# Prompt attention: where the value products stand in each quarter of TensorE's program

## The reference, cut to what matters

```python
lg = jnp.einsum('bqghd,bwgd->bghqw', qs, k_win) + tab[t5_bucket(d_win)].transpose(2, 3, 0, 1)
p_win = masked_softmax(lg, m_win)
o_win = jnp.einsum('bghqw,bwgd->bqghd', p_win.astype(v_win.dtype), v_win)
g = jax.nn.sigmoid(gts.astype(jnp.float32)).astype(q.dtype)[..., None]
return g[:, :, 0] * o_cmp + g[:, :, 1] * o_sel + g[:, :, 2] * o_win
```

## Time and profile before

| what | value |
|---|---|
| median of three runs | 1658.26 us (1655.5 to 1662.54) |
| profiled execution, its own time | 1658.38 us |
| its span | 1656.5 us |
| PE busy over the span | 1527.3 us (92%), 10098 matmuls |
| DVE, ACT, POOL busy | 720.8 us, 605.5 us, 201.3 us |
| prompt attention, window 865 to 1346 us | 481 us, PE busy 462.08 |
| granted TensorE clock, mean | 0.969 of full speed |

### The profile page before, as it was taken

One profiled execution on the slowest core, in us unless ns is written; L12 is line 12 of the kernel. 1 busy time (PEld: TensorE's weight loads), 2 busy tenths in 40 slices (PEclk: granted clock), 3 DMA queues, 4 the chain that ended last, 5 costly groups with the idle time before them and its releaser, 6 DMA issues.

```text
span 1656.5 us, 25563 instructions
## 1 busy us (share of the span) xinstructions
PE 1527.3 (92%) x10098; PEld 1321.3 (80%) x10098; DVE 720.8 (44%) x1773; ACT 605.5 (37%) x1231; POOL 201.3 (12%) x380
## 2 busy tenths in 40 slices
PE   5997999999999999959959999999999988799996
PEld 1887999999999999958847777777777766588884
DVE  2540221313123131245557677667676654543221
ACT  2430111110111111124456676666666645521110
POOL 1104000000000000021011122122121131000000
PEclk9999999999999999979979999999999999799998
DMA  9707432332222323187120121111011049662320
GB/s 345 127 27 270 114 103 78 78 90 65 77 78 69 99 53 89 40 267 242 57 85 26 33 75 30 31 44 39 27 47 32 20 152 292 205 193 91 100 67 20
DMA packets 164936, 164.62 MB, mean 99 GB/s; under 512 B 48685, under 2 KB 146029, under 8 KB 159505
## 3 DMA queue, kind: packets, MB, share of 16 engines
q1 hardware_dynamic: 150800, 96.66, 21.9%
q0 software_dynamic: 14016, 66.32, 11.8%
HBM read 131.27 MB, written 35.83 MB: 101 GB/s over the span
## 4 chain that ended last, share of the span: by engine, by line
PE 84%; DVE 6%; DMA 5%; ACT 2%; issue 2%; SPq 1%; POOL 0%; DVEq 0%; ACTq 0%; POOLq 0%
PE PS L975 33%; PE PS L1314 11%; PE PS L1130 8%; PE PS L1098 7%; PE PS L1076 4%; PE PS L1023 4%; PE PS L1077 3%; DMA wr<-in_w_in 2%; PE PS L937 1%; PE PS L938 1%; PE PS L939 1%; PE PS L1170 1%; DMA wor<-in_w_out 1%; DMA adaw<-in_ada_w 1%; PE PS L1015 1%
## 5 line engine op out<-in xcount | busy, mean ns | idle before, releaser
L975 PE MATMUL PS<-hhi,wh 128*128 128x352 f32 x1152 | 251.2, 326 | 9.1 <-issue 8.5
L975 PE MATMUL PS<-hhi,wl 128*128 128x352 f32 x1152 | 248.7, 323 | 0.0
L975 PE MATMUL PS<-hlo,wh 128*128 128x352 f32 x1152 | 248.4, 324 | 0.0
L1479 ACT ACTIVATE pr<-PS,nm 128x640 f32<-128x640 f32 (+7 forms) x256 | 179.8, 704 | 81.9 <-DVE nm L1815 78.1
L975 PEld LDWEIGHTS PS<-hhi,wh 128*128 128x128 f32 x1152 | 196.0, 189 | 13.0 <-issue 11.6
L975 PEld LDWEIGHTS PS<-hhi,wl 128*128 128x128 f32 x1152 | 198.2, 188 | 0.0
L975 PEld LDWEIGHTS PS<-hlo,wh 128*128 128x128 f32 x1152 | 196.0, 188 | 0.0
L1499 ACT ACTIVATE ptt<-PS 128x512 f32<-128x512 f32 x222 | 128.0, 596 | 73.0 <-PE PS L1098 72.8
L1098 PE MATMUL PS<-ident,pr 128*128 128x128 f32 x1056 | 147.3, 274 | 0.0
L1692 DVE TENSOR_TENSOR wl<-wr,wh 128x1024 fp32r<-128x1024 f32 x48 | 58.6, 1220 | 187.5 <-ACT wh L1395 187.0
L1130 PE MATMUL PS<-ptt,kvt 128*64 128x256 f32 x1056 | 136.1, 389 | 1.1 <-DVE ptt L1855 0.7
(11 more groups left out here) (317 smaller groups left out, 2314.2 us busy)
## 6 DMA issues: line engine op xcount, KB each, us to landing
wr<-in_w_in SPq DMA_DIRECT2D x32, 512.0 KB, 7.6
adaw<-in_ada_w SPq DMA_DIRECT2D x8, 1024.0 KB, 9.7
wr<-in_w_in SPq DMA_DIRECT2D x32, 256.0 KB, 3.7
qb<-q_stacked SPq DMA_DIRECT2D x32, 256.0 KB, 3.1
mr<-mixed SPq DMA_DIRECT2D x16, 512.0 KB, 3.9
mixed<-ych POOLq DMA_DIRECT2D x8, 528.0 KB, 3.3
z_attn_silu<-zab POOLq DMA_DIRECT2D x8, 528.0 KB, 2.9
xb<-in_x_prompt POOLq DMA_DIRECT2D x8, 512.0 KB, 7.8
```

Of the source, the lines that this page charges most:

```text
L975: ins = pe.matmul(PS[:, bank + c, 0:CH], a[kind % 2][:, k, :], b[:, k, c * CH:(c + 1) * CH], start=(k == 0 and b is hhi and a is wh), stop ...
L1479: act.activation(pr[r][:, h, 0:k], score_cols(b0, w), ACT.Exp, scale=-1.0, bias=nm[:, r, h:h + 1], accum_out=rsum[:, r, h:h + 1]).then_inc ...
```

## The change

In each quarter `values` moves from behind the turns to a place between the scores and the turns (and ahead of `turn_factors`). In the last two quarters all tiles held are taken, whatever their number; as the quarter's own tiles are not turned yet at that point, these are the tiles of earlier quarters. In the first two quarters it is, as before, the tiles of the window before. The other engines' programs are the same.

```diff
                 for h, part in enumerate(slots(w)):
                     if w + 2 < NI:
                         scores(w + 2, h)
+                    go = sum(x[0] < w for x in held) if h < 2 else len(held)
+                    for x in held[:go]:
+                        values(*x)
+                    held = held[go:]
                     if w % 2 and h == 0:
                         turn_factors(w // 2)
                     for t in part:
                         turn_p(w, t)
                         held.append((w, t))
-                    old = [x for x in held if x[0] < w]
-                    go = len(old) if h < 2 else len(held) - 1 if len(held) >= 5 else 0
-                    for x in held[:go]:
-                        values(*x)
-                    held = held[go:]
             for x in held:
                 values(*x)
```

## The result

The changed kernel takes 1709.21 us (median of four runs, 1702.72 to 1715.84) against 1656.9 us for the kernel before in the same comparison: a ratio of 1.0305 with a 95% interval of 1.0281 to 1.0329. It is 52 us slower. The direction was forecast, the size was not: I had said 1683 us and a range up to 1700.

What follows compares the result with a forecast made beforehand. PE alone was taken to set the pace with large tiles. +10.9 + 11.4 + 2 - 3.0 = +21.3 us there and +4 for small ones made +25 us on 1658.26: 1683 us, range 1660 to 1700.

Steps and rivals of the forecast that it cites:

- The visits: Runs of value products between other PE work: 100 become 168, 0.33 us each before, 0.30 after; +10.9 large, +6.5 small tiles.
- the rival with the full drain: Every entry into value products from scores pays the dearer price, 13.4 us more in all: 1697 us, chance 0.08.
- The 0.17 us from turns to values: Cost of entering value products behind eight transposes: 0.96 us when values follow against 0.79 when scores follow.
- The wait for sel_ev: Odd windows' first product, right behind the third quarter's scores, waits for DVE's selected_o: +11.4 us large tiles, 10.6 small.
- r_ev: Even windows' first product waits for it; the rest of the second quarter and the third's scores hide it: no cost.
- The copies: Values of tiles turned in the same quarter no longer wait for DVE's copy: 3.0 us gone.
- the end of those rows as a sign of being right: In the chain of waits, rows of L1130 (value products) waiting for ptt would be gone.
- Bank waits and small windows: Scores' 16.8 us of bank waits absorb most of 6.5 us visits and 10.6 us sel_ev: +4 us, bounds -17 and +17.
- The 2 us for late exponentials in large windows: ACT's exponentials come later and are wanted sooner: an eighth of a microsecond in 16 even windows, bounds 0 and 5.

Runs made afterwards that it cites:

- the two experiments on them: Changed kernel with values issued behind the turns again: 1679.11 us, ratio 1.0113; kernel before with half the products between a quarter's two turns: 1673.26 us, ratio 1.0097.
- newest held back: Changed kernel, but tiles turned in the quarter just before wait one quarter longer and the first two quarters issue values behind the turns: 1685.57 us, ratio 1.0155.

## Why the prediction was wrong in size

**The visits: right.** The counts are 100 and 168. Both prices show up in the kernel after, here in window 6 (timeline of PE):

```profile
919.58 0.39 PE L1076 MATMUL PS<-ksh,qb 128*128 128x512 f32 x1
919.81 0.40 PE L1077 MATMUL PS<-ksl,qb 128*128 128x512 f32 x1
920.14 0.65 PE L1130 MATMUL PS<-ptt,kvt 128*64 128x256 f32 x4
920.72 1.09 PE L1098 MATMUL PS<-ident,pr 128*128 128x128 f32 x8
921.57 0.42 PE L1076 MATMUL PS<-kwh,qb 128*128 128x384 f32 x1
```

From scores to values it is 0.33 us where scores follow each other by 0.23: 0.10 us to enter, also behind 512 columns, where I had 0.09 from 384. That decides against the rival with the full drain. The Trainium skill (TensorEngine Tiling, Key Properties) says that a change of tiling mode drains the TensorE: the trace agrees that each change costs. The Trainium skill's page TensorE: Matmul & The Clock Gate (Single matmul latency) gives about 175 ns for a drain; the 0.10 us measured here is less. The eight turns behind a visit take 0.85 us against 0.79: 0.06, where I had 0.05. So the visits are +17 us as summed, and the two experiments on them, +19 us for 68 and +14.6 us for 48, fit. One reading in the sum was right only as a whole. The 0.17 us from turns to values, against turns to scores, is not a dearer entry: the transposes start 0.11 us apart (0.44 for four), so eight in 0.79 us mean that scores start some 0.03 us behind the last one, and their first product then takes longer (kernel before):

```profile
912.70 0.48 PE L1076 MATMUL PS<-ksh,qb 128*128 128x512 f32 x1
913.02 0.40 PE L1077 MATMUL PS<-ksl,qb 128*128 128x512 f32 x1
```

That is 0.32 us where 0.23 is usual. In the old order the scores behind a visit take 0.34 us there, nearly the same, so 0.33 us a visit stays right. Split visits stand between turns and have no such scores to compare with, so their expectation came out 0.08 us too high.

**The wait for sel_ev: right, and partly taken by another wait.** Window 7 in the kernel after (PE and DVE):

```profile
925.53 0.60 PE L1098 MATMUL PS<-ident,pr 128*128 128x128 f32 x4
...
925.73 0.56 DVE L1813 TENSOR_REDUCE nm<-PS 128x1 f32<-128x384 f32 x1
...
926.06 0.45 PE L1076 MATMUL PS<-kwh,qb 128*128 128x384 f32 x1
...
926.73 0.42 DVE L1861 TENSOR_TENSOR mixs<-PS,fac 128x256 f32<-128x256 f32 x1
926.75 0.28 PE L1077 MATMUL PS<-kwl,qb 128*128 128x256 f32 x1
...
927.30 1.52 PE L1130 MATMUL PS<-ptt,kvt 128*64 128x256 f32 x12 [0.27 <-DVE mixs L1861]
```

The chain is as long as before: minima at 925.73, selected_o 1.00 us later, as in the earlier trace rows. The product starts 0.15 us after it ends. It starts 0.55 us behind the last scores product, where 0.21 is usual behind 256 columns: 0.34 us of waiting by starts, of which the profile shows 0.27, where I had 0.54. The missing 0.2 us went before it: four transposes took 926.06 - 925.53 = 0.53 us instead of 0.35, a wait of 0.18 us for a bank; PE's own row doesn't list it, the row of the weights does (0.17 us, released by ACT pr). Of the eight odd windows with i of 6 and 7, four look like this one; in the other four the bank wait is 0.67 us by starts (0.42 listed), and then PE doesn't wait for selected_o at all. I had summed 11.4 us for large tiles and 10.6 for small ones. Worked out by starts, window by window, it is 6.4 and 9.7, 16 us (the listed 12.4 leave out short ones, four that are listed under ptt, and what modelled ends cover). With the newest held back, where the copies don't interfere, it is 11.5 and 10.8, very nearly my sum. Taking the wait away gave 8.

**r_ev: wrong.** I put it at nothing, with the rest of the second quarter as cover. The profile has four such waits, 3.4 us: 0.36 us twice at i=5 and 1.33 us twice at i=1, where a window has two tiles, its quarters are short, so that less of PE's work covers near_o.

**The copies: the step that failed.** The prediction said that values of tiles turned in the same quarter waited for DVE's copy and booked 3.0 us as gone. It named the end of those rows as a sign of being right. It did not ask what is late next, so the new wait stood at nothing without a reason. Once nothing is held back, the newest tile was turned just before, and only one head's scores lie between its turn and its product. The one length of such scores in the prediction, 1.0 us, is that of the large windows. While the units shrink (i = 5, 3, 1) the scores are those of smaller windows, 0.3 to 0.8 us, and a turn, its copy and the product need 1.34 us. I had also put the wait for selected_o into the same third quarters without asking for the copies behind it. The term is +20 us on PE's waits and 24 us by the experiment that removes it, instead of -3. The difference, 27 us, is about what the forecast was short by (26 us), but that it fits so well is luck, as other terms were off both ways (below).

**Bank waits and small windows: right in kind, too large.** I let the small windows absorb most of their visits and sel_ev for +4 us, which takes 13 us out of the bank waits. They fell by 8.4 us as listed, and by some 4 as worked out by starts. Where the rest of the loss lies is seen from the starts of selected_o (line 1862 before, 1861 after), in us from unit to unit, means over the eight-unit rounds:

```
interval that ends in the unit with i =   2     4     6     7     5     3     1     0
before                                  14.2  18.1  19.9  20.0  17.1  12.7   8.8   9.4
after                                   15.4  18.3  21.2  21.2  18.7  15.7  12.2  10.6
newest held back                        14.7  17.9  21.0  21.0  17.7  13.8  10.2  10.6
```

The intervals of i = 5, 3 and 1 lose 1.6, 3.0 and 3.4 us each time, and get 1.0, 1.9 and 2.0 of it back once the newest tiles are held. The intervals of i = 6 and 7 lose 1.2 to 1.3 us, which is what visits and sel_ev were said to cost there.

**The 2 us for late exponentials in large windows** are in the bank waits at i = 6 and 7 told above, 0.18 or 0.67 us by starts in each odd window. They cost little more there: with the wait for selected_o it is 0.52 or 0.67 us a window, where selected_o alone was summed at 0.54.

**The sum.** The listed waits on PE rose by 26 us, what PE stands idle in the stage by 27 (18.7 to 45.5), and its busy time by 26, of which the visits are 17. The rest of the busy time hides waits under modelled ends. My estimate by starts over the whole stage, with the undelayed distances (to values 0.33, 0.27 and 0.21 us behind scores of 512, 384 and 256 columns and 0.20 behind a transpose), places it: visits 18, copies 21, selected_o 16, r_ev 4, and 4 less before scores are 55, against 53 measured. Against my sum the copies are 24 us more and the bank waits 9 (13 taken out, 4 gone), r_ev is 4 more, selected_o 6 less and the late exponentials 2 less.

## What to carry to other kernels

When a consumer is moved nearer to its producer, list for every stage of the loop what still stands between them, and compare it with the whole chain (turn, copy, product), not with the engine's idle share: engines 60 to 65% busy can form a ring in which all wait. A split and a move that cost little by themselves can cost most together, since one takes the slack that the other used. The number of mode changes has a best value: in this kernel both fewer and many more were slower, and a few more in the right windows were faster. Count them at 0.3 us, but check what a longer run does to the engines that it starves.

## What was not expected of the hardware

A change of the weights from 128 by 128 to 128 by 64 costs about the same behind everything that was seen here: 0.10 us behind scores of 512 columns, 0.09 behind 384, and 0.09 between transposes (0.53 against 0.44 us for four). The 0.17 us that a comparison of starts gives behind transposes counts a start of the scores that comes early and is paid for by their first product. The change back costs 0.16 us, and 0.06 us more if transposes follow. And idle time before a matmul, as the profile gives it, leaves out waits up to some 0.4 us behind a run of transposes (1.18 us for eight that take 0.79), so that small waits have to be read from starts.
